# Two transformer blocks on one core: first tiles, turns, the RWKV chain and the bias map in another order, and five spare matmuls in each norm

## The chip, the cores and the metric

The kernel runs on one core of one Trainium2 chip. A core has a matrix engine (TensorE, PE in the profile), VectorE (DVE), ScalarE (ACT), GpSimd (POOL) and SyncE (SP), which here only issues transfers. Each engine works through its own list of instructions in order, and semaphores make one wait for another. The metric is the device time of one execution in microseconds; less is better.

## The reference

Two blocks in a row, on 256 tokens of width 1024, with fp32 inputs and outputs. The first block is of depth 2 and carries a second stream, 256 tokens of context, through nearly all of it. Cut to what matters here:

```python
def first_block(x, c, ctx, c_ctx, ...):
    h, hc = x, ctx
    for l in range(DEPTH):                     # DEPTH = 2
        # nine shift, scale and gate vectors for each stream: silu(c) @ w_ada[l] + b_ada[l]
        h = h + 0.5 * g1 * _swiglu(_modulate(_rms_norm(h, norm_ffn1[l]), sh1, sc1), ...)   # up1, down1
        # the same for hc
        u = _modulate(_rms_norm(h, norm_mix[l]), shm, scm)                                  # in
        # 16 heads: window, global and neighbourhood attention, each over its keys and the context's
        h = h + gm * (jnp.concatenate([y_w, y_g, y_n], axis=-1) @ w_out[l])                 # out
        h = h + 0.5 * g2 * _swiglu(_modulate(_rms_norm(h, norm_ffn2[l]), sh2, sc2), ...)   # up2, down2
    return _rms_norm(h, norm_final)

def second_block(x, positions, rel_bias, ...):
    h = _rmsnorm(x, norm_mix[l])
    p_rwkv, p_mla, p_diff, p_gate = jnp.split(h @ w_in[l], IN_SPLITS, axis=-1)
    o_rwkv = _rwkv7_mix(p_rwkv, ...)
    o_mla = _mla_mix(p_mla, ...)
    o_diff = _diff_mix(p_diff, positions, rel_bias, ...)
    x = x + merged @ w_o[l]                    # merged: the three, each by its gate
    x = x + _conv_ffn(_rmsnorm(x, norm_ffn[l]), ...)                                        # up_2, down_2
    return _rmsnorm(x, norm_final)

# inside _diff_mix
dist = positions[:, q0:q1, None] - positions[:, None, :q1]
bias = rel_bias[_t5_bucket(dist)]              # 32 buckets, 4 heads
logits = q @ k * scale + bias
```

## The kernel before, in words

**Weights.** Every fp32 product is made of three matmuls (`three`, L1083 to L1085) on operands that are split in a high and a low part: high by high, low by high, high by low. The weights come in panels of 128 x 2048 or less through one stream. SP issues the load of a panel (`Stream.load`), ACT writes the high part (`whi`, L537, in pieces L552 and L554), DVE the low part (`wlo`, L539, in pieces L560), PE multiplies. In places where PE works on attention a panel is split in quarters (`quarter`, L578, L592) between other instructions. `Stream.run` (L597) carries the phases up1, down1, up2, down2, w_o, up_2 and down_2: in each group of panels it evacuates the results of the group before, has the next panel split, and multiplies. The first panel of the next phase is split beside the last group. With `early` the second panel of a phase is taken to be split already by someone else.

**Norms.** `norm_scale` (L926) sums the squares over all features by matmuls with a table of ones (L937, L940), takes the root and the reciprocal, makes diagonal matrices of them (L956) and spreads these over all partitions by a matmul with ones (L964). `norm` (L981) then makes the normed operand `u` chunk by chunk (8 chunks of 128 features) as `u_hi` and `u_lo`. A chunk of both streams goes the wide way (L1017, L1044, L1047, L1052), the first chunk the slim way (L1009, L1025, L1035, L1036). PE starts on a chunk when its `u_lo` is there.

**In phases and attention of the first block.** `in_tile(i)` computes one output tile of `u @ w_in` over the 8 chunks; `program` runs them in an order with the attention of the heads between them. The results are evacuated by ACT from L1384 on. A list of heads' steps runs as generators, which are turned one step at a time. DVE's L1644 scales the probabilities; ACT and DVE prepare what PE multiplies. The w_out tiles follow at the end.

**The bias map.** The relative bias of the diff attention, a map of 128 x 4 heads x 384, is made by POOL alone in `bias_map` (L1224), from the list's place in layer 1 on: two DMAs (L1227, L1228), two casts, a distance (L1238), a start value (L1243), and for each of 31 bucket borders and 4 heads a pair: L1247 writes (distance >= border) x step into `bucket_step`, L1250 adds that to `rel_bias_map`. Each of the 248 instructions waits for the one before it. DVE adds the causal mask in L2227.

**Second block.** POOL's `load` (L1762) issues four DMAs: the tables, `w_a_g`, `pos_row_m` and, much later, `uq_ukv`. The RWKV part has three stages. First the chain (L1981 to L2189): token shifts, the small low-rank products, decay, norms of the keys, bonus, with DVE, ACT and PE handing each other small tiles; `v_tokens` (L2017) is the squared keys, whose sums over features PE makes in L2028; L2114 is the bonus. Its last DVE operation `e1` (L2189) starts the second stage, an inverse by six levels of small matmuls (L2184) with additions on DVE (L2220). Third, the scan over the chunks of the sequence (from L2291 on PE), which waits for a state set to zero by DVE (L2234). After the levels DVE does L2227, then L2234. In all of these stages `dense(n)` puts n quarter panels of side products, the panels of `w_in` for diff, MLA and gates, between the steps, so that PE has work while it waits. Their number is fixed: what is done early is missing at the end of the diff and MLA attention.

Nothing plans the order at run time: each engine's instructions stand in the order in which the program's functions are called.

## Time and profile before

| | us |
|---|---|
| median of 3 runs | 2553.18 (2553.05 to 2558.97) |
| the profiled execution | 2550.05 |
| its span, first to last instruction | 2548.7 |
| PE busy | 2408.7 (95%) |
| weight loads of PE busy | 1979.8 (78%) |
| DVE busy | 1210.2 (47%) |
| ACT busy | 970.3 (38%) |
| POOL busy | 441.2 (17%) |
| mean granted clock of PE | 0.972 of 2.4 GHz |

Places of the stages on the profile's time axis: attention of layer 0 from 500 to 700 us, norm and first in tiles of layer 1 from 1500 to 1525, attention of layer 1 from 1540 to 1700, up2 and down2 of layer 1 to 1926, norm to 1940, RWKV chain to 2037, levels to 2091, scan to 2131, diff and MLA attention to 2250, then gates and w_o to 2325, up_2 to 2471, down_2 to the end.

How to read it. A busy time of PE counts the time that matmuls are in the engine, so it holds no waiting but doesn't say whether they ran at full clock; the granted clock (1.00 is 2.4 GHz, 0.50 is 1.2 GHz) does. "Idle before" is the time for which an engine had nothing to do ahead of an instruction, and "<-" names what ended that wait. The chain is followed back from the last instruction, at each step to what released it.

### The profile page before, as it was taken

How to read it: one execution, taken by the hardware profiler on the slowest of the kernel's cores; microseconds unless marked ns; L12 is line 12 of the kernel's file. 1: busy time of each engine (PE TensorE's matmuls, PEld its weight loads, DVE VectorE, ACT ScalarE, POOL GpSimd, SP SyncE). 2: the span in 40 equal slices, each digit the busy share in tenths (PEclk: the TensorE clock that was granted, in tenths of full speed). 3: DMA queues.
4: the chain of work that ended last, by engine and by line, in shares of the span. 5: the costliest groups of instructions: out<-in, count | busy, mean ns of one | idle time of the engine just before them, and what ended most of it. 6: DMA issues, size and time to landing. Idle time of an engine off the chain costs nothing.

```text
span 2548.7 us, 38444 instructions
## 1 busy us (share of the span) xinstructions
PE 2408.7 (95%) x15464; PEld 1979.8 (78%) x15464; DVE 1210.2 (47%) x1797; ACT 970.3 (38%) x1540; POOL 441.2 (17%) x318
## 2 busy tenths in 40 slices
PE   7999999999999999999999989879988899998988
PEld 4777777666667777778888866669987897798988
DVE  4333222545653323243333346566655755676764
ACT  4222212455442222242222244345435324555762
POOL 1000000100000000000000039999994000000000
PEclk9999999899999999999999989999998899999999
DMA  7554455311034444323222241114544221244444
GB/s 281 209 182 176 160 200 184 97 50 50 34 132 168 179 177 164 136 85 115 90 92 84 96 117 67 66 67 158 178 148 143 84 105 55 84 149 149 170 151 141
DMA packets 51943, 329.51 MB, mean 129 GB/s; under 512 B 6480, under 2 KB 7504, under 8 KB 20976
## 3 DMA queue, kind: packets, MB, share of 16 engines
q1 hardware_dynamic: 48608, 318.46, 35.1%
q0 software_dynamic: 3216, 9.36, 1.3%
q8 instruction: 87, 1.43, 0.2%
q14 instruction: 32, 0.26, 0.0%
HBM read 323.99 MB, written 3.80 MB: 129 GB/s over the span
## 4 chain that ended last, share of the span: by engine, by line
PE 81%; DVE 8%; ACT 7%; issue 2%; DMA 2%; SPq 0%; ACTq 0%; DVEq 0%
PE bank L1083 24%; PE bank L1084 22%; PE bank L1085 22%; DVE wlo L539 2%; PE bank L825 2%; PE bank L1658 1%; PE bank L1591 1%; ACT sil L1044 1%; ACT whi L537 1%; PE bank L1680 1%; PE bank L2184 1%; DMA first_ada<-in_stream 1%; ACT u_hi L1047 1%; ACT probs L1628 1%; ACT probs_t L1665 1%
## 5 line engine op out<-in xcount | busy, mean ns | idle before, releaser
L1083 PE MATMUL bank<-u_hi,whi 128*128 128x512 f32 (+1 forms) x2512 | 882.3, 351 | 39.4 <-DVE wlo L539 13.2
L1084 PE MATMUL bank<-u_lo,whi 128*128 128x512 f32 (+1 forms) x2512 | 860.2, 342 | 0.0
L1085 PE MATMUL bank<-u_hi,wlo 128*128 128x512 f32 (+1 forms) x2512 | 858.5, 342 | 0.0
L1083 PEld LDWEIGHTS bank<-u_hi,whi 128*128 128x128 f32 x2512 | 485.8, 193 | 140.9 <-issue 50.6
L539 DVE TENSOR_TENSOR wlo<-raw,whi 128x2048 fp32r<-128x2048 f32 (+2 forms) x213 | 435.1, 2044 | 302.9 <-ACT whi L537 302.6
L1085 PEld LDWEIGHTS bank<-u_hi,wlo 128*128 128x128 f32 x2512 | 486.5, 194 | 53.1
L1084 PEld LDWEIGHTS bank<-u_lo,whi 128*128 128x128 f32 x2512 | 486.9, 194 | 47.8 <-issue 0.2
L537 ACT ACTIVATE whi<-raw 128x2048 fp32r<-128x2048 f32 (+2 forms) x213 | 360.9, 1695 | 171.1 <-PE bank L1085 118.2
L1145 ACT ACTIVATE sil<-bank 128x512 f32<-128x512 f32 (+1 forms) x88 | 47.9, 545 | 619.7 <-PE bank L1085 619.6
L1149 DVE TENSOR_TENSOR prod<-sil,bank 128x512 f32<-128x512 f32 (+1 forms) x88 | 54.7, 621 | 460.0 <-ACT sil L1145 456.9
L1247 POOL TENSOR_SCALAR bucket_step<-distance,bucket_steps 128x384 f32<-128x384 f32 x124 | 251.9, 2031 | 12.6
L1297 POOL DMA_DIRECT2D tables<-in_const x2 | 1.2, 580 | 1348.1 <-PE bank L1085 1348.1
L1083 PE MATMUL bank<-hidden_hi,whi 128*128 128x512 f32 x528 | 210.5, 399 | 0.0
L1085 PE MATMUL bank<-hidden_hi,wlo 128*128 128x512 f32 x528 | 208.4, 395 | 0.0
L1084 PE MATMUL bank<-hidden_lo,whi 128*128 128x512 f32 x528 | 208.3, 395 | 0.0
L1250 POOL TENSOR_TENSOR rel_bias_map<-rel_bias_map,bucket_step 128x384 f32<-128x384 f32 x124 | 146.8, 1184 | 10.3
L889 ACT ACTIVATE prod<-h 128x512 f32<-128x512 f32 (+3 forms) x63 | 33.4, 537 | 270.3 <-DVE h L1188 259.0
L560 DVE TENSOR_TENSOR wlo<-raw,whi 128x1024 fp32r<-128x1024 f32 (+1 forms) x70 | 89.1, 1280 | 75.9 <-ACT whi L552 63.1
L1083 PEld LDWEIGHTS bank<-hidden_hi,whi 128*128 128x128 f32 x528 | 99.3, 188 | 31.0 <-issue 7.4
L1085 PEld LDWEIGHTS bank<-hidden_hi,wlo 128*128 128x128 f32 x528 | 99.3, 188 | 23.6
L1084 PEld LDWEIGHTS bank<-hidden_lo,whi 128*128 128x128 f32 x528 | 99.3, 188 | 22.8
L1188 DVE SCALAR_TENSOR_TENSOR h<-bank,mod_g,h 128x256 f32<-128x256 f32 (+1 forms) x94 | 41.9, 479 | 128.1 <-PE bank L1085 128.0
(418 smaller groups left out, 2940.2 us busy)
## 6 DMA issues: line engine op xcount, KB each, us to landing
raw<-in_stream SPq DMA_DIRECT2D x231, 1024.0 KB, 4.8
raw<-in_stream SPq DMA_DIRECT2D x80, 704.0 KB, 4.0
first_ada<-in_stream SPq DMA_DIRECT2D x8, 1024.0 KB, 17.0
raw<-in_stream SPq DMA_DIRECT2D x8, 768.0 KB, 4.4
skew<-rpb_rows POOLq DMA_DIRECT2D x8, 336.0 KB, 6.6
nbr_bias<-skew POOLq DMA_DIRECT2D x24, 112.0 KB, 4.0
h<-in_tokens SPq DMA_DIRECT2D x1, 2048.0 KB, 12.0
uq_ukv<-in_small POOLq DMA_DIRECT2D x1, 1536.0 KB, 6.8
```

Source lines behind the costliest of these rows:

```text
L537: a.activation(self.hi[to][:, 0:n], raw[:, 0:n], ACT.Copy).then_inc(self.s_hi, 1)
L539: v.tensor_tensor(self.lo[to][:, 0:n], raw[:, 0:n], self.hi[to][:, 0:n].bitcast(F32), ALU.subtract).then_inc(self.s_lo, 1)
L560: r = v.q.tensor_tensor(self.lo[to][:, cols], self.raw[slot][:, cols], self.hi[to][:, cols].bitcast(F32), ALU.subtract)
L825: r = pe.q.matmul(banks[6][32 * q:32 * q + 32, 0:256], csil[:, 2 * k + i, :], weights[:, i * D + q * 256:i * D + q * 256 + 256], start=(k ...
L1083: pe.q.matmul(dst, w[0], x[0], start=start, stop=False)
L1084: pe.q.matmul(dst, w[0], x[1], start=False, stop=False)
L1085: return pe.q.matmul(dst, w[1], x[0], start=False, stop=stop)
L1145: act.q.activation(sil[par][:, 0:n], banks[2 * par][:, 0:n], ACT.Silu).then_inc(s_sil, 1)
L1149: dve.q.tensor_tensor(prod[par][:, 0:n], sil[par][:, 0:n], banks[2 * par + 1][:, 0:n], ALU.mult).then_inc(st.s_ev, 1)
L1188: r = dve.q.scalar_tensor_tensor(out=h[:, m, lo:hi], in0=bank[:, lo:hi], scalar=gate(s), in1=h[:, m, lo:hi], op0=ALU.mult, op1=ALU.add)
L1247: z = pool.do(pool.q.tensor_scalar(bucket[:, :], dist[:, :], float(start), steps[:, hh, b + 1:b + 2], ALU.is_ge, ALU.mult))
L1250: z = pool.do(pool.q.tensor_tensor(rel[:, hh, :], rel[:, hh, :], bucket[:, :], ALU.add))
```

## The change

1. **Loads.** SP issues `pos_row_m`, `w_a_g` and the tables, behind the first two panels of RWKV's `w_in`; POOL issued them before, behind the map. `uq_ukv` stays on POOL. All of SP's loads are put at the end of the program's text; their order on SP is otherwise as it was.
2. **Heads of down phases.** With `ahead`, the phase before splits the second panel in four pieces before its last evacuation; every down phase is `early`.
3. **Norms.** `stay_busy` puts matmuls on constants into a bank that nobody reads: 1 behind the sums of the kept squares, 1 behind the sums of the last ones, 3 behind the spreading matmuls, in 7 norms. In norms of two streams groups 0, 3 and 6 are slim, where only group 0 was.
4. **First tiles.** `first_tiles` runs the first two in tiles of a layer chunk by chunk side by side; the first side panel of the second block does the same.
5. **Bias map.** Its arithmetic starts only when the second panel of w_out in layer 1 is multiplied. The first 20 borders (80 pairs) stand there; the last 11 (44 pairs) are issued behind `e1`.
6. **RWKV chain.** The sines and cosines come first, the sigmoid ahead of the tanh, the key scaling `kk0` ahead of the decay's exponential, two of four reciprocals earlier, and five more quarters of dense work stand in the chain and at the beginning of the diff attention.

```diff
-    def load_rest(self):
+    def load_rest(self, second_block):
...
+            if ph.name == "rwkv_in":
+                second_block()
...
+        if ahead:
+            for piece in (0, 1, 2, 3):
+                self.split_piece(after, 1, piece)
         evacuate(Count(m), (g0 + m) % 2, Count(g0 + m), done)
...
+    def stay_busy(bank, times):
+
+        for _ in range(times if bank is not None else 0):
+            pe.q.matmul(banks[bank][:, 0:S], cst("ones"), const[:, 0:S], start=True, stop=True)
...
         for x in parts:
             sums(x, ssq, True, False)
+        stay_busy(spare, 1)
...
+        stay_busy(spare, 1)
         marks = [None, None]
         for x in parts:
             pe.after(scaled[x])
             marks[x] = pe.do(pe.q.matmul(banks[4 + x][:, 0:S], cst("ones"), diag[:, x * S:(x + 1) * S], start=True, stop=True))
+        stay_busy(spare, 3)
...
-            par, slim = x % 2, x < narrow
+            par, slim = x % 2, x < narrow or (streams == 2 and x % 3 == 0)
...
-        st.run(name, multiply, evacuate, ppg=2)
+        st.run(name, multiply, evacuate, ppg=2, early=True)
...
-        pool.after((s_pos, 32))
+        pool.after((s_pos, 32), (st.s_pe, PHASE[("out", L1 - 1)].first + 2))
...
-        for b, start in enumerate(bucket_starts()):
+        return bias_steps(z, 0, 20)
+
+    def bias_steps(z, lo, hi):
+
+        for b in range(lo, hi):
+            start = bucket_starts()[b]
             for hh in range(DH):
...
+        def first_tiles():
+
+            n = [q_cols(kind) for kind, _ in IN_TILES[0:2]]
+            places = [next_bank() for _ in n]
+            pe.q.wait_ge(st.s_lo, in_first + 1)
+            for kc in range(KC):
+                pe.after(ready[kc])
+                first = three(places[0][1][:, 0:n[0]], tile_of(in_first % 2, kc), chunk_of(u, kc, 0, n[0]), kc == 0, kc == KC - 1)
+                if kc == KC - 1:
+                    half_done = pe.do(first)
+                second = three(places[1][1][:, 0:n[1]], tile_of(in_first % 2, KC + kc), chunk_of(u, kc, 0, n[1]),
+                               kc == 0, kc == KC - 1)
+            second.then_inc(st.s_pe, 1)
...
-    tab2_ready = load(tab[:, :], ins["const"][:, CC.at["causal"]:CC.n], hidden_free)
...
+    def second_block_tables():
+        sp.wait_ge(*hidden_free)
+        sp.dma_start(prow[:, :], ins["pos_row"]).then_inc(s_row_pos, 16)
+        sp.dma_start(wag[:, :], ins["small"][:, SM_WA:SM_N]).then_inc(s_wag, 16)
+        sp.dma_start(tab[:, :], ins["const"][:, CC.at["causal"]:CC.n]).then_inc(s_tab2, 16)
...
+    trig_done = angles()
     for i in range(4):
         dense(2)
...
+    dve.after(*[mixed[c] for c in range(4, 8)])
+    for c in range(4):
+        kk0 = dve.do(dve.q.tensor_scalar(kk[:, c, :], K_[:, c, :], vcol("k_k", c), None, ALU.mult))
     act.after(sg)
-    trig_done = angles()
     dc = act.do(act.q.activation(flat4(dec[:, :, :]), flat4(dec[:, :, :]), ACT.Exp, scale=-float(np.exp(-0.5))))
...
     sqk = act.do(act.q.activation(flat4(vT[:, :, :]), flat4(kk[:, :, :]), ACT.Square))
-    dense(2)
-
+    dense(4)
...
+    dve.after(scanned, z1)
+    pinv = [dve.do(dve.q.reciprocal(by_chunk(dec[:, :, :])[:, c, :, :], Pb[:, c, :, 1:CH + 1])) for c in range(2)]
     dense(3)
...
     e1 = dve.do(dve.q.tensor_tensor(v16(TT[:, :, :]), ident_rows, v16(Mm), ALU.subtract))
+    pool.after(e1)
+    map_ready = bias_steps(map_ready, 20, NBUCKET - 1)
     dense(2)
...
-        dense(1 + i % 2)
+        dense(1 + i % 2 + (i < 2))
```

What stands in the engines' lists, at three places. Line numbers differ between the kernels, since the text has moved.

PE, the norm ahead of the in phase of layer 1, from its last sums to the first tile, before:

```order
L937 MATMUL bank<-const,prod 128x1
L937 MATMUL bank<-const,prod 128x1 [waits act_done]
L937 MATMUL bank<-const,prod 128x1
L964 MATMUL bank<-inv_norm_diagonal,const 128x256 [waits dve_done] x2
L1083 MATMUL bank<-u_hi,whi 128x256 [waits dve_done,weights_lo_done]
L1084 MATMUL bank<-u_lo,whi 128x256
L1085 MATMUL bank<-u_hi,wlo 128x256
L1083 MATMUL bank<-u_hi,whi 128x256 [waits dve_done]
L1084 MATMUL bank<-u_lo,whi 128x256
L1085 MATMUL bank<-u_hi,wlo 128x256
L1083 MATMUL bank<-u_hi,whi 128x256 [waits dve_done]
```

The tile's three matmuls of a chunk are followed by a wait for the next chunk.

PE at the same place in the changed kernel, where L933 is a spare matmul:

```order
L933 MATMUL bank<-const 128x256
L946 MATMUL bank<-const,prod 128x1 [waits act_done]
L946 MATMUL bank<-const,prod 128x1
L946 MATMUL bank<-const,prod 128x1 [waits act_done]
L946 MATMUL bank<-const,prod 128x1
L933 MATMUL bank<-const 128x256
L975 MATMUL bank<-inv_norm_diagonal,const 128x256 [waits dve_done] x2
L933 MATMUL bank<-const 128x256 x3
L1094 MATMUL bank<-u_hi,whi 128x256 [waits dve_done,weights_lo_done]
L1095 MATMUL bank<-u_lo,whi 128x256
L1096 MATMUL bank<-u_hi,wlo 128x256
L1094 MATMUL bank<-u_hi,whi 128x512
```

Spare matmuls (L933) stand ahead of, between and behind the norm's own, and the first chunk's three matmuls for one tile are followed by three for the second tile (128x512) before the next chunk is waited for.

POOL, the end of its list, before:

```order
L1250 TENSOR_TENSOR rel_bias_map<-rel_bias_map,bucket_step 128x384 [waits pool_done]
L1247 TENSOR_SCALAR bucket_step<-distance,bucket_steps 128x384 [waits pool_done]
L1250 TENSOR_TENSOR rel_bias_map<-rel_bias_map,bucket_step 128x384 [waits pool_done]
L1766 DMA tables_11689<-in_const 128x704 [waits panel_multiplied]
L1766 DMA w_a_g<-in_small 128x1024
L1766 DMA pos_row_m<-in_pos_row 128x256
L1766 DMA uq_ukv<-in_small 128x3072 [waits dve_done,act_done,pe_done]
```

The loads wait behind the map's last pair.

POOL in the changed kernel around the 81st pair, of which L1263 is the step of a bucket and L1266 its addition to the map:

```order
L1266 TENSOR_TENSOR rel_bias_map<-rel_bias_map,bucket_step 128x384 [waits pool_done]
L1263 TENSOR_SCALAR bucket_step<-distance,bucket_steps 128x384 [waits pool_done]
L1266 TENSOR_TENSOR rel_bias_map<-rel_bias_map,bucket_step 128x384 [waits pool_done]
L1263 TENSOR_SCALAR bucket_step<-distance,bucket_steps 128x384 [waits pool_done,dve_done]
L1266 TENSOR_TENSOR rel_bias_map<-rel_bias_map,bucket_step 128x384 [waits pool_done]
```

The 81st pair waits for DVE (`dve_done`, which stands for `e1`); three of the four loads have left POOL's list, and the last one stands behind the map as before.

DVE, the end of the levels and the beginning of the scan, before:

```order
L2220 TENSOR_TENSOR inverse_t<-inverse_t,bank 128x512
L2227 TENSOR_TENSOR rel_bias_map<-rel_bias_map,tables_11689 128x4x128 [waits tokens_loaded,constants_loaded,pool_done]
L2227 TENSOR_TENSOR rel_bias_map<-rel_bias_map,tables_11689 128x4x128
L2234 MEMSET sil 128x256 [waits dve_done]
L539 TENSOR_TENSOR wlo<-raw,whi 128x2048 [waits weights_hi_done]
```

The map is added to right behind the last level.

DVE at the same place in the changed kernel:

```order
L541 TENSOR_TENSOR wlo<-raw,whi 128x2048 [waits weights_hi_done]
L2258 TENSOR_TENSOR inverse_t<-inverse_t,bank 128x512 [waits pe_done]
L2258 TENSOR_TENSOR inverse_t<-inverse_t,bank 128x512
L2265 TENSOR_TENSOR rel_bias_map<-rel_bias_map,tables_10966 128x4x128 [waits tokens_loaded,constants_loaded,pool_done]
L2265 TENSOR_TENSOR rel_bias_map<-rel_bias_map,tables_10966 128x4x128
L2275 MEMSET sil 128x256 [waits dve_done]
```

The two additions to `rel_bias_map` wait for POOL in both kernels, stand at the same place, and the memset of the state and the next split of weights stand behind them.

## Rows read from the trace of the kernel before

**Rows 1.** the page, busy times and the chain that ended last, by engine.
```profile
PE 2408.7 (95%) x15464; PEld 1979.8 (78%) x15464; DVE 1210.2 (47%) x1797; ACT 970.3 (38%) x1540; POOL 441.2 (17%) x318
...
PE 81%; DVE 8%; ACT 7%; issue 2%; DMA 2%; SPq 0%; ACTq 0%; DVEq 0%
```

**Rows 2.** stretches: us, busy us (x instructions), PE clock, DMA share, GB/s.
```profile
1730.00:1853.00 123.00, 123.00 (x1028) 123.00 (x1027) 74.11 (x66) 53.02 (x66) 117.07 (x65) 1.00 0.51 180
1940.00:2037.00 97.00, 81.91 (x793) 78.26 (x793) 65.20 (x120) 42.61 (x70) 3.39 (x5) 0.88 0.30 109
2037.00:2091.00 54.00, 54.00 (x1148) 51.93 (x1145) 27.60 (x30) 15.09 (x21) 0.00 (x0) 1.00 0.22 76
```

**Rows 3.** timeline of POOL, 1505 to 1521 us: start, duration, instruction [idle before <-releaser].
```profile
1513.27 0.73 POOL L1231 CAST bucket_step<-pos_row 128x256 f32<-128x256 int32 x1 [3.54 <-DMA pos_col<-in_pos_col]
...
1520.24 1.58 POOL L1247 TENSOR_SCALAR bucket_step<-distance,bucket_steps 128x384 f32<-128x384 f32 x1
```

**Rows 4.** instruction groups, POOL, 1520 to 1942 us: busy, mean | idle.
```profile
L1247 POOL TENSOR_SCALAR bucket_step<-distance,bucket_steps 128x384 f32<-128x384 f32 x124 | 251.9, 2031 | 12.6
L1250 POOL TENSOR_TENSOR rel_bias_map<-rel_bias_map,bucket_step 128x384 f32<-128x384 f32 x124 | 146.8, 1184 | 10.3
```

**Rows 5.** groups of instructions, POOL, 1598 to 1609 us.
```profile
L1247 POOL TENSOR_SCALAR bucket_step<-distance,bucket_steps 128x384 f32<-128x384 f32 x4 | 6.3, 1582 | 0.4
L1250 POOL TENSOR_TENSOR rel_bias_map<-rel_bias_map,bucket_step 128x384 f32<-128x384 f32 x4 | 4.0, 1002 | 0.3
```

**Rows 6.** groups of instructions, POOL, 1730 to 1853 us.
```profile
L1247 POOL TENSOR_SCALAR bucket_step<-distance,bucket_steps 128x384 f32<-128x384 f32 x33 | 76.0, 2304 | 3.4
L1250 POOL TENSOR_TENSOR rel_bias_map<-rel_bias_map,bucket_step 128x384 f32<-128x384 f32 x32 | 42.5, 1327 | 2.7
```

**Rows 7.** timeline of DVE, 2089.8 to 2093.2 us.
```profile
2091.10 1.29 DVE L2227 TENSOR_TENSOR rel_bias_map<-rel_bias_map,tables 128x512 f32<-128x512 f32 x2
```

**Rows 8.** timeline of PE at the end of w_out's second panel, layer 1.
```profile
1696.01 0.28 PE L1085 MATMUL bank<-y_hi,wlo 128*128 128x256 f32 x1
```

**Rows 9.** timeline of DVE at e1, 2036 to 2037.3 us.
```profile
2036.13 1.23 DVE L2189 TENSOR_TENSOR inverse_t<-tables,mixed 128x1024 f32<-128x1024 f32 x1
```

**Rows 10.** groups of instructions, DVE, 1730 to 1853 us.
```profile
L539 DVE TENSOR_TENSOR wlo<-raw,whi 128x2048 fp32r<-128x2048 f32 (+1 forms) x21 | 48.9, 2331 | 26.8 <-ACT whi L537 26.8
L1128 DVE TENSOR_TENSOR hidden_x_lo<-prod,hidden_x_hi 128x256 f32 (+1 forms) x22 | 17.6, 798 | 0.5 <-ACT hidden_x_hi L1126 0.5
```

**Rows 11.** groups of instructions, DVE, 2037.36 to 2091.1 us.
```profile
L539 DVE TENSOR_TENSOR wlo<-raw,whi 128x2048 fp32r<-128x2048 f32 x4 | 9.2, 2289 | 5.5 <-ACT whi L537 5.5
...
L2178 DVE TENSOR_TENSOR mixed<-chunk_products,tables 128x1024 f32<-128x1024 f32 x5 | 6.1, 1224 | 6.9 <-PE bank L2184 6.9
```

**Rows 12.** groups of instructions, PE, 1503 to 1525 us.
```profile
L1083 PE MATMUL bank<-u_hi,whi 128*128 128x256 f32 (+1 forms) x18 | 8.8, 487 | 7.6 <-DVE u_lo L1052 5.6 <-DVE u_lo L1036 2.1
```

**Rows 13.** busy time of the engines in three stretches at a lower clock.
```profile
1503.00:1525.00 22.00, 14.95 (x53) 11.68 (x54) 12.21 (x21) 14.00 (x27) 17.31 (x24) 0.61 0.50 112
1974.00:1985.00 11.00, 9.91 (x48) 9.94 (x49) 7.43 (x24) 5.49 (x9) 0.00 (x0) 0.53 0.00 1
2005.00:2015.00 10.00, 6.65 (x24) 5.64 (x23) 9.93 (x20) 0.09 (x1) 0.00 (x0) 0.50 0.29 107
```

**Rows 14.** timeline of PE, head of the down phase of layer 1.
```profile
1857.19 0.39 PE L1083 MATMUL bank<-hidden_x_hi,whi 128*128 128x256 f32 x1 [2.08 <-DVE wlo L539]
```

**Rows 15.** timeline of PE, head of the last down phase.
```profile
2476.25 0.58 PE L1083 MATMUL bank<-hid,whi 128*128 128x256 f32 x1 [4.92 <-DVE wlo L539]
```

**Rows 16.** groups of instructions, PE, 1969.1 to 1978.6 us.
```profile
L2028 PE MATMUL bank<-const,v_tokens 128*128 128x2 f32 x16 | 3.5, 351 | 6.1 <-ACT v_tokens L2017 6.1
```

**Rows 17.** groups by shape, DVE, attention of layer 1, 1540 to 1700 us.
```profile
L1644 DVE TENSOR_SCALAR probs<-probs,stat 128x512 f32<-128x512 f32 x32 | 21.3, 707 | 0.6
```

**Rows 18.** groups by shape, DVE, attention of layer 0, 500 to 700 us.
```profile
L1644 DVE TENSOR_SCALAR probs<-probs,stat 128x512 f32<-128x512 f32 x32 | 14.1, 483 | 0.6
```

**Rows 19.** groups of instructions, PE, 1926 to 1940 us, a norm.
```profile
L964 PE MATMUL bank<-inv_norm_diagonal,const 128*128 128x256 f32 x4 | 1.8, 584 | 0.6 <-DVE inv_norm_diagonal L956 0.6
```

82 lines of the change are left out of this document (41 added, 41 removed).

## The prediction

> **What bounds the kernel now.** I read the page's busy times and its chain first [rows 1]. TensorE (PE) is busy 95% of the span and holds 81% of the chain that ended last; VectorE (DVE) holds 8% and ScalarE 7%. So time can be gained only where PE waits or runs at its lower clock, and it is lost wherever another engine makes PE wait longer. GpSimd (POOL) is busy 17%, and all of that matters little today. Then I read the stretches [rows 2]: from 1730 to 1853 us PE has no gap and POOL works beside it almost without a pause; from 1940 to 2037, the RWKV chain, PE is busy 82 of 97 us at clock 0.88; from 2037 to 2091, the inverse by levels, PE is full and POOL does nothing. The change puts POOL work into exactly that last stretch, so I next followed POOL's bias map.
>
> The map is built by 124 pairs (31 buckets x 4 heads) of L1247 and L1250, each instruction waiting for the one before. They start at 1520.24 [rows 3] and end at 1941.8, and with the idle time before them they take 251.9 + 146.8 + 12.6 + 10.3 = 421.6 us, 3.40 us a pair [rows 4]. The rate differs by place: with little on DVE a pair takes (6.3 + 4.0 + 0.4 + 0.3) / 4 = 2.75 us [rows 5]; with DVE busy 60% it takes (76.0 + 42.5 + 3.4 + 2.7) / 32.5 = 3.83 us [rows 6]. The first reader of the map is DVE's L2227, which starts at 2091.10 [rows 7]. Before, the map is ready 149 us ahead of it.
>
> **The map.** The changed kernel starts the map when the second w_out panel of layer 1 is multiplied, 1696.01 + 0.28 = 1696.3 [rows 8]. Setup takes 1520.24 - 1513.27 = 7.0 us [rows 3], so pairs start at about 1703. Eighty pairs at 3.40 to 3.83 us take 272 to 306 us and end at 1975 to 2009. The 81st pair waits for DVE's e1 (L2189), which ends at 2036.13 + 1.23 = 2037.4 [rows 9]; even if what follows moves e1 forward by 20 us, POOL will mostly be standing idle there, for 10 to 60 us.
> From e1 on 44 pairs remain, and DVE's L2227 stands 2091.10 - 2037.36 = 53.7 us behind it. Both instants shift together, so this distance is what the map can hide in. In it DVE is busy 51% [rows 2], close to the stretches that give the mean of 3.40; I take that: 53.7 / 3.40 = 15.8 pairs are covered. The other 28.2 run while DVE is stopped at L2227 with its split of the weights queued behind it, so PE soon has nothing either. They run at the free rate of 2.75 us: **78 us**. The bounds: all 44 at the free rate, 44 x 2.75 - 53.7 = 67 us; the slow rate of 3.83 for the covered part, (44 - 53.7 / 3.83) x 2.75 = 82 us, and 85 at 4.1 us a pair in the covered part, a little above [rows 6]. Queued behind L2227 on DVE are the state's memset and every weight split; PE's scan waits for the memset, so PE stops after the two quarter panels of dense work placed ahead of the scan. PE comes back from a 70 us pause at its lower clock, which costs 3 us (1 to 4), taken from the stretches below in which it restarts at 0.50 to 0.53.
>
> The row on which a rule can be weighed: POOL spends 118.5 us on 32.5 pairs where it would need 32.5 x 2.58 = 84, thus 35 us lost, beside DVE instructions with two inputs in on-chip memory that are busy 48.9 + 17.6 = 66.5 us [rows 6, 10]. The Trainium skill, SBUF — State Buffer, section "Who interferes with whom", says that such a DVE instruction and a GpSimd one that reads this memory share a port pair which is an exclusive lock, and that the later one blocks fully. By a full lock POOL would have lost up to 66.5 us; the trace shows about half, so it agrees in kind and not in size. By the full rule the DVE instructions of that sort among the levels, 9.2 + 6.1 = 15.3 us [rows 11], would leave 38.4 us or 14 pairs, and a stall of 83 us instead of 78; by the half that the trace shows, 75 us.
>
> **What it gains.**
> In-phases. The first two tiles are interleaved chunk by chunk, so that each normed chunk feeds two tiles. In layer 1 PE stands 7.6 us between 1503 and 1525 waiting for u_lo [rows 12] and runs at 0.61 [rows 13]. I take 11 us over both layers and the RWKV head (8 to 14), since the work of the second tile, some 6 us a layer, goes into gaps.
> Heads of the down phases. Their first panel now is split ahead. PE waits 2.08 us for wlo at 1857.19 [rows 14] and 4.92 at 2476.25 [rows 15], 7.0 in all, and comes back with matmuls of 0.39 and 0.58 us against 0.28 before the pause; with that restart and layer 0: 10 us (7 to 11).
> RWKV chain. PE waits 6.1 us for ACT's v_tokens [rows 16] and then runs at 0.53 from 1974 to 1985, later at 0.50 from 2005 to 2015 [rows 13]. The busy time there, 9.9 + 6.7, would be half at full clock. So 6.1 + 8.3 = 14.4 is at stake, with a short wait beside it, and a few more quarters of dense work and earlier tables and reciprocals go there: 15 us (6 to 20). The five quarters are taken from the end of the diff and MLA attention, where fewer remain as cover: 0 (-5 to +4).
> Attention of layer 1. Without POOL beside it DVE's L1644 takes 483 ns, as in layer 0, and not 707 [rows 17, 18]: 32 x 0.22 = 7.2 us of DVE time, and as much again in its other lines. PE idles there more than in layer 0 and runs at a lower clock; I take 7 us (0 to 14).
> Norms. Spare matmuls, 35 in all, keep PE busy while it waits; one is like L964, 584 ns at the low clock [rows 19]. Most lie in time that is idle; the three behind the broadcast can delay the first real matmul by up to 1.5 us a norm. Together with the slimmer groups: 5 us (-4 to +13).
> The DMAs moved from POOL to SP, w_a_g, tables_2 and pos_row_m, would arrive before 1950 as before: 0. The uq_ukv load now stands behind the map, at its end, and is wanted only in the diff and MLA part, over 40 us later: 0.
> The sum: 11 + 10 + 15 + 7 + 5 = 48 us gained; 78 + 3 = 81 us lost; net +33 us. On the profiled 2550.05 us (a span of 2548.7) that is 2583; the profiled run stood 3.1 us under the median of 2553.18, so on the median I forecast **2586 us**.
>
> **The rivals.**
> 1. The gains mostly don't come (spare matmuls delay real ones, the chain still waits for v_tokens, the clock falls anyway). Against it: the waits named are plain and their releasers are moved earlier. With 20 us gained: 2553 + 81 - 20 = 2614.
> 2. The gains are at their upper ends and the rest of the map runs at its free rate: 67 + 2 - 65 = +4, some 2557 to 2563. For it: each removed wait also keeps the clock up. Against it: the terms would all have to go the same way.
> 3. The map is hidden after all, and the kernel is faster. The mechanism: from e1 to L2227, the 44 pairs fit, so that only the gains count, 2553 - 48 = 2505. It decides at 53.7 / 44 = 1.22 us a pair; L1247 alone takes 1.58 where it is free [rows 5]. It could only be so if DVE's wait were met earlier than the last pair, and the order of instructions shows it behind pool_done. A weaker form, where the wait is passed on and the pause is then given back by weights that are already split and loaded, can return no more than a few us, since PE is 95% busy.
> 4. The 81st pair comes late because POOL has not finished the first 80 at e1. At 4.1 us a pair (above [rows 6]) they end at 2031, and with e1 earlier by 20 us that adds up to 14 us: 2600. For it: DVE is busy 67% of the RWKV chain [rows 2]. Against: the mean rate leaves 28 us of room.
>
> **Chances.** Forecast, with rival 4's smaller part: 0.60, its own range 2571 to 2602. Rival 1: 0.16. Rival 4 in full: 0.06. Rival 2: 0.11, of which 0.03 falls within 0.3% (7.7 us, about what a measurement can tell) and 0.02 below. Rival 3: 0.04. Something between the forecast and 2560 for other reasons: 0.03, counted as slower. This gives slower 0.90, same 0.04, faster 0.06. The range reaches from 2559 to 2614; it takes in the bounds of the stall (67 to 85) with gains of 25 to 62.
>
> **What would show it.** In the changed kernel's trace: POOL starts at 1690 to 1700 and not at 1513; its 81st pair starts right after DVE's e1 with an idle time of 10 to 60 us released by DVE; DVE has an idle time of 70 to 85 us before the first rel_bias_map add, released by POOL; PE has one pause of about 70 us or more before the scan, the longest of the kernel; L1644 in layer 1 takes about 480 ns; the wait for v_tokens falls below 3 us; the waits for wlo at the heads of the down phases are gone. The forecast is wrong if the pause before the scan is under 50 us, which would mean that the pairs run faster among the levels than anywhere now, or if it is there and the total is nonetheless under 2560, which would mean gains that I have undercounted.

## The result and the profile after

| | before | after |
|---|---|---|
| median | 2553.11 us (4 runs) | 2620.99 us (2619.91 to 2621.96, 4 runs) |
| profiled execution | 2550.05 | 2621.4 |
| its span | 2548.7 | 2620.1 |
| mean granted clock of PE | 0.972 | 0.965 |

The ratio is 1.0263, with a 95% interval of 1.0244 to 1.0281: 67 us slower. I had forecast 2586 and a range of 2559 to 2614. The direction is right, the size is half of what it was, and the time lies outside the range.

The page of the changed kernel, its busy times and the chain that ended last, which answer to [rows 1]:

```profile
PE 2416.7 (92%) x15534; PEld 1984.7 (76%) x15534; DVE 1200.3 (46%) x1822; ACT 962.3 (37%) x1534; POOL 435.4 (17%) x315
...
PE 75%; DVE 9%; ACT 7%; POOL 5%; issue 2%; DMA 1%; ACTq 0%; DVEq 0%; SPq 0%; POOLq 0%
```

POOL was in no place of the chain before and now holds 5% of it. Where, the windows show, which answer to [rows 2]: the RWKV norm and chain (111 us before, 1926 to 2037), the levels, and what follows them.

```profile
1908.00:2028.00 120.00, 95.98 (x882) 90.72 (x883) 81.43 (x138) 51.09 (x88) 60.21 (x41) 0.86 0.27 96
2028.00:2083.00 55.00, 54.82 (x1148) 52.71 (x1144) 29.42 (x30) 14.92 (x20) 51.92 (x32) 1.00 0.22 79
2083.00:2162.00 79.00, 0.93 (x8) 0.72 (x6) 2.34 (x4) 0.00 (x0) 73.16 (x58) 0.53 0.04 13
```

In the last 79 us PE is busy 0.9 us and POOL 73. That is the stop that I had forecast. DVE's and PE's timelines show both ends of it (start, duration, instruction, idle time before it and what ended that):

```profile
2160.82 1.29 DVE L2265 TENSOR_TENSOR rel_bias_map<-rel_bias_map,tables 128x512 f32<-128x512 f32 x2 [76.66 <-POOL rel_bias_map L1266]
2162.11 0.27 DVE L2275 MEMSET sil<- 128x256 f32 x1
```

PE's timeline at the first matmul of the scan:

```profile
2162.53 0.38 PE L2332 MATMUL bank<-v_tokens,chunk_products 64*64 64x64 f32 x2 [78.60 <-DVE sil L2275]
```

DVE waits 76.66 us for POOL's last pair and PE 78.60 us for the memset behind it; [rows 7] had no wait. POOL's own timeline shows that the arithmetic starts at 1680.29 and not at 1513.27 [rows 3]:

```profile
1680.29 0.40 POOL L1242 CAST bucket_step<-pos_row 128x256 f32<-128x256 int32 x1 [173.06 <-PE bank L1096]
```

The same view at the 81st pair, which starts at `e1` after 56.31 us of idle time:

```profile
2028.22 4.59 POOL L1263 TENSOR_SCALAR bucket_step<-distance,bucket_steps 128x384 f32<-128x384 f32 x1 [56.31 <-DVE inverse_t L2225]
```

POOL's groups of instructions for the first 80 pairs (busy, mean ns | idle before), which answer to [rows 4]:

```profile
L1263 POOL TENSOR_SCALAR bucket_step<-distance,bucket_steps 128x384 f32<-128x384 f32 x80 | 165.3, 2066 | 8.1
L1266 POOL TENSOR_TENSOR rel_bias_map<-rel_bias_map,bucket_step 128x384 f32<-128x384 f32 x80 | 104.5, 1306 | 6.7
```

And for the last 44:

```profile
L1263 POOL TENSOR_SCALAR bucket_step<-distance,bucket_steps 128x384 f32<-128x384 f32 x44 | 76.0, 1726 | 60.7 <-DVE inverse_t L2225 56.3
L1266 POOL TENSOR_TENSOR rel_bias_map<-rel_bias_map,bucket_step 128x384 f32<-128x384 f32 x44 | 48.6, 1104 | 3.7
```

The first 80 take (165.3 + 104.5 + 8.1 + 6.7) / 80 = 3.56 us each and are done 56.3 us before e1 ends. The last 44 take 76.0 + 48.6 + (60.7 - 56.3) + 3.7 = 132.7 us, 3.02 each: from e1's end at 2028.2 to the levels' end at 2084.2 DVE gives 56.0 us of cover, and 132.7 - 56.0 = 76.7 us remain.

So the stop came as worked out (78 us). What did not come are the gains. To read them I compared the times at which the profiled executions of the two kernels reach the same instruction. The changed kernel is ahead by 5.6 us at the first attention, 2.5 at the norm before in of layer 1 (1501.2 to 1498.7), 16.3 at the norm after w_out, 19.6 at the norm before RWKV, and then only 9.2 at e1 and 7.0 at the last level. At the end it is 71.4 behind: 78.6 for the stop and less than 8 gained. Inside the chain PE stands still for 22.3 us, in four places, each time waiting for split weights (the shortest, 1.85 us, is not shown). Its timeline at the first:

```profile
1935.13 0.58 PE L1094 MATMUL bank<-u_hi,whi 128*128 128x256 f32 x1 [8.09 <-DVE wlo L541]
```

At the second, which begins 36 us after the end of the first:

```profile
1978.59 0.58 PE L1094 MATMUL bank<-u_hi,whi 128*128 128x256 f32 x1 [7.56 <-DVE wlo L541]
```

And at the last, behind the bonus:

```profile
2002.39 0.58 PE L1094 MATMUL bank<-u_hi,whi 128*128 128x256 f32 x1 [4.82 <-DVE wlo L541]
```

The wait for `v_tokens` [rows 16] has indeed shrunk, from 6.1 to 0.27 us, and the waits for weights have taken its place.

### The profile page after: what moved, and what is told of

It is laid out like the page before. It is cut to its first block, busy times and chain, and to the rows that moved or that the text cites. A ratio compares the mean times of both kernels' runs of the same rounds, so it can differ in the third digit from the quotient of the medians.

```text
span 2620.1 us, 38607 instructions
## 1 busy us (share of the span) xinstructions
PE 2416.7 (92%) x15534; PEld 1984.7 (76%) x15534; DVE 1200.3 (46%) x1822; ACT 962.3 (37%) x1534; POOL 435.4 (17%) x315
## 4 chain that ended last, share of the span: by engine, by line
PE 75%; DVE 9%; ACT 7%; POOL 5%; issue 2%; DMA 1%; ACTq 0%; DVEq 0%; SPq 0%; POOLq 0%
PE bank L1094 22%; PE bank L1095 21%; PE bank L1096 21%; POOL bucket_step L1263 3%; PE bank L829 3%; DVE wlo L541 2%; POOL rel_bias_map L1266 2%; PE bank L1693 1%; ACT sil L1056 1%; PE bank L1715 1%; PE bank L1626 1%; ACT whi L539 1%; ACT u_hi L1059 1%; DMA first_ada<-in_stream 1%; ACT probs L1663 1%
## 5 line engine op out<-in xcount | busy, mean ns | idle before, releaser
L541 DVE TENSOR_TENSOR wlo<-raw,whi 128x2048 fp32r<-128x2048 f32 (+2 forms) x208 | 426.9, 2053 | 305.5 <-ACT whi L539 305.3
L539 ACT ACTIVATE whi<-raw 128x2048 fp32r<-128x2048 f32 (+2 forms) x208 | 354.3, 1703 | 175.0 <-PE bank L1096 127.1
L1263 POOL TENSOR_SCALAR bucket_step<-distance,bucket_steps 128x384 f32<-128x384 f32 x124 | 241.2, 1946 | 68.8 <-DVE inverse_t L2225 56.3
L1266 POOL TENSOR_TENSOR rel_bias_map<-rel_bias_map,bucket_step 128x384 f32<-128x384 f32 x124 | 153.0, 1234 | 10.3
L562 DVE TENSOR_TENSOR wlo<-raw,whi 128x1024 fp32r<-128x1024 f32 (+2 forms) x80 | 92.1, 1171 | 97.5 <-ACT whi L554 81.8
```

The lines of the kernel that those rows point to most:

```text
L539: a.activation(self.hi[to][:, 0:n], raw[:, 0:n], ACT.Copy).then_inc(self.s_hi, 1)
L541: v.tensor_tensor(self.lo[to][:, 0:n], raw[:, 0:n], self.hi[to][:, 0:n].bitcast(F32), ALU.subtract).then_inc(self.s_lo, 1)
L562: r = v.q.tensor_tensor(self.lo[to][:, cols], self.raw[slot][:, cols], self.hi[to][:, cols].bitcast(F32), ALU.subtract)
L1263: z = pool.do(pool.q.tensor_scalar(bucket[:, :], dist[:, :], float(start), steps[:, hh, b + 1:b + 2], ALU.is_ge, ALU.mult))
L1266: z = pool.do(pool.q.tensor_tensor(rel[:, hh, :], rel[:, hh, :], bucket[:, :], ALU.add))
```

## The experiments

All ratios are to the kernel before on the same chip, with 95% intervals.

### The map alone, and the rest alone

**map_on_before**: the map's two edits in the kernel before.

```diff
-        pool.after((s_pos, 32))
+        pool.after((s_pos, 32), (st.s_pe, PHASE[("out", L1 - 1)].first + 2))
...
+    pool.after(e1)
+    map_ready = bias_steps(map_ready, 20, NBUCKET - 1)
```

> The kernel before with the change to the bias map alone: arithmetic from w_out's second panel on, the last 44 pairs behind e1. Theory A, the stopped pairs alone make the loss and their price adds to the rest: DVE waits 76 to 80 us for POOL before the first rel_bias_map add, some 6 us are lost in levels, restart and scan, some 6 are gained in layer 1's attention where POOL is gone: 2553 + 78 + 6 - 6 = 2631, 2622 to 2638. Theory B, part of the 77 us pause in the changed kernel was given back by work done ahead and the loss comes from elsewhere: under 2610.

Measured: 2659.46 us, 1.0421 (1.0405 to 1.0437), above what either theory gave. The stop is there with nearly the same length, as DVE's timeline shows:

```profile
2197.51 1.29 DVE L2234 TENSOR_TENSOR rel_bias_map<-rel_bias_map,tables 128x512 f32<-128x512 f32 x2 [78.62 <-POOL rel_bias_map L1255]
```

But there is a second one. PE's groups of instructions between 1945 and 1985:

```profile
L1991 PE MATMUL bank<-mixed,w_a_g 64*128 64x256 f32 x8 | 3.8, 648 | 32.8 <-issue 32.8
```

And POOL's timeline just behind the 80th pair:

```profile
1976.91 0.55 POOL L1771 DMA_DIRECT2D w_a_g<-in_small  x1
```

PE stands 32.8 us until `w_a_g` is there: the profile names no releaser ("issue"), but the load lands 4.1 us after it was issued, at 1981.0, and PE goes on at 1981.2. The load stands on POOL's list behind the first 80 pairs, which now end at 1976 and not at 1942. In the changed kernel SP issues this load at 1906.5, and PE does not wait for it. The move of the loads to SP, which I had booked at 0, thus belongs to the map's move: without it the 32.8 us come on top.

**map_early**: the changed kernel with the map's arithmetic where and as it was. **late_whole**: the start at w_out kept, the gate at e1 taken away.

```diff
# map_early; late_whole keeps the first line of "-"
-        pool.after((s_pos, 32), (st.s_pe, PHASE[("out", L1 - 1)].first + 2))
+        pool.after((s_pos, 32))
...
-        return bias_steps(z, 0, 20)
+        return bias_steps(z, 0, NBUCKET - 1)
...
-    pool.after(e1)
-    map_ready = bias_steps(map_ready, 20, NBUCKET - 1)
```

> The changed kernel with the map's arithmetic as it was before (from in layer 1's list on, all 124 pairs in one piece, no wait for e1). Theory A: no wait of DVE for POOL; 2621 - 77 - 6 + 6 = 2544, 2539 to 2550, so faster than before by 0.3 to 0.4 per cent only, since the RWKV chain gives nothing. Theory B, the other parts gain the 48 us that I forecast and something else is lost with the map: 2505 to 2520.

> The changed kernel with the map in one piece from w_out's second panel on, no wait for e1, the reader where it is. In the changed kernel POOL stands 56.3 us at e1; without that the 44 pairs move into the chain, where they run at 3.4 to 3.8 us. Theory A, the gate costs what it takes from POOL: the map ends at 1687 + 124 x 3.5 = 2121, some 37 us behind the levels' end at 2084: 2621 - 77 + 37 = 2581, 2572 to 2590. Theory B, POOL beside the chain slows DVE as much as it hides: over 2600.

Measured: map_early 2547.24 us, 0.998 (0.9971 to 0.9989); late_whole 2577.69 us, 1.0095 (1.0077 to 1.0113). Theory A held in both. The map's late start and gate together cost (1.0263 - 0.998) x 2553 = 72 us, what the late start gains in the attention taken off, and all other parts together gain 5 us. DVE's timeline of late_whole at the map's reader:

```profile
2119.73 1.29 DVE L2263 TENSOR_TENSOR rel_bias_map<-rel_bias_map,tables 128x512 f32<-128x512 f32 x2 [29.90 <-POOL rel_bias_map L1266]
```

Of the 76.7 us, 46.8 are therefore the gate's and 29.9 the late start's. In total 43 us went with the gate.

**add_late26**: 26 borders before e1, 5 behind it, and the first reader moved behind the scan.

```diff
-    dve.after(map_ready, tab2_ready, loaded)
-    for o in (0, 2 * P):
-        rel_ready = ...
...
+    dve.after(map_ready, tab2_ready, loaded)
+    for o in (0, 2 * P):
+        rel_ready = ...
     dve.after(rel_ready, lam_ready, scan_over)
```

> The changed kernel with 26 of the 31 borders before e1 and 5 behind it, and the causal mask added to the map (the first reader) only before the diff attention, behind the scan. Theory A, the loss is only that the reader stands before the last pair: no pause before the scan; 20 pairs at 2.8 to 3.4 us end 56 to 68 us behind e1, long before the diff attention: 2621 - 77 - 4 = 2540, 2534 to 2547, at or under map_early. Theory B, POOL's pairs beside the DVE work of the chain and the scan cost as much as beside the attention: 2545 to 2555.

Measured: 2548.05 us, 0.9984 (0.9975 to 0.9993). The stop is gone: the last pair ends at 2119.5, and the reader, which now stands behind the scan, starts at 2138.3. Two things were changed here, the reader's place and six more borders ahead of e1, and no run has the first alone. By my estimate it would not do: 44 pairs of 3.02 us from e1's end at 2034.8 on would end at 2168, 30 us behind that reader. And the kernel is no faster than map_early, though it is 15.9 us ahead of the kernel before at the norm after w_out and map_early only 5.4. By e1 that is down to 2.5 against 3.9. Theory B is nearer.

### The RWKV chain

**chain_back_map_early**: map_early with the chain of before.

```diff
-    trig_done = angles()
     for i in range(4):
...
     act.after(sg)
+    trig_done = angles()
...
-    pinv = [...reciprocal... for c in range(2)]
...
-    dense(5)        # and 3, 4, and (i < 2) in the diff attention
+    dense(4)        # and 2, 3, without (i < 2)
```

> As map_early, and the RWKV chain of before in it: sines behind the decay's sigmoid, tanh ahead of sigmoid, kk0 late, all four reciprocals behind bb, the quarters of dense work as before. Theory A, the new order of the chain is what costs there (in the changed kernel PE stands still 8.1, 7.6, 1.9 and 4.8 us in it, 22.3 in all, against 15.1 before): 10 to 20 us faster than map_early, 2524 to 2534. Theory B, the late weights come from the loads that SP now issues behind the end of down2: no faster than map_early, 2540 to 2548, and e1 no earlier than in it.

Measured: 2531.34 us, 0.9918 (0.9905 to 0.9932), as theory A had it. The new chain costs 16 us. Four kernels divide that.

**angles_late** puts back the place of the sines alone, **rest_back** all but that, **quarters_back** the numbers of quarters alone:

```diff
# angles_late, on map_early
-    trig_done = angles()
     for i in range(4):
...
     act.after(sg)
+    trig_done = angles()
# quarters_back, on map_early (rest_back has this too)
-    dense(5)
+    dense(4)
...
-            dense(3)
+            dense(2)
...
-    dense(4)
+    dense(3)
...
-        dense(1 + i % 2 + (i < 2))
+        dense(1 + i % 2)
```

> map_early with one thing put back: the sines and cosines behind the decay's sigmoids, as before. Theory A, the early sines are the main cost of the new chain: ACT stands 8.0 us at the first sine until DVE has the angles, its split of the third RWKV panel waits behind that, and PE stands 8.1 us for it. 2547 - 8 to 12 = 2535 to 2539. Theory B, the dense work, the reciprocals and kk0 cost it: 2544 to 2548.

> map_early with the other things of the chain put back (tanh first, kk0 late, four reciprocals behind bb, the quarters of dense work in the chain and in the attentions as before) and the sines still first. Theory A as above: 2547 - 3 to 6 = 2541 to 2544. Theory B: 2532 to 2537.

> map_early with the five quarters of dense work alone put back (4, 2 and 3 in the chain instead of 5, 3 and 4, and none extra in the first two units of the diff attention); sines, kk0 and two reciprocals stay early. Theory A, the quarters cost the 15 us between map_early (2547) and rest_back (2532): a quarter needs a weight panel that DVE has split, and in the chain DVE is the engine that is behind, so PE waits for wlo: 2531 to 2536. Theory B, the two reciprocals (1.7 us each on DVE, ahead of the norm of the keys) cost it: 2543 to 2548. In between, both share.

Measured: angles_late 2546.15 us, 0.9976 (0.9967 to 0.9985); rest_back 2532.07 us, 0.9919 (0.9905 to 0.9932); quarters_back 2536.26 us, 0.993 (0.9917 to 0.9944). My theory of the sines fell: their place is worth 1 us. They do make a pause: with them first, PE waits 7.95 us for the third panel (rest_back), because ACT stands at the first sine until DVE has the angles, and its split of the weights is behind that. With them late, PE waits 6.06 us for `v_tokens` (chain_back_map_early). One wait is exchanged for another. PE's timeline of rest_back:

```profile
1942.36 0.58 PE L1094 MATMUL bank<-u_hi,whi 128*128 128x256 f32 x1 [7.95 <-DVE wlo L541]
```

And of chain_back_map_early:

```profile
1963.26 0.56 PE L2066 MATMUL bank<-const,v_tokens 128*128 128x2 f32 x2 [6.06 <-ACT v_tokens L2052]
```

The quarters are 11 to 13 of the 15 us (by the medians and by the ratios). **three_more** adds only three quarters to the good chain:

```diff
-    dense(4)
+    dense(5)
...
-            dense(2)
+            dense(3)
...
-    dense(3)
+    dense(4)
```

> chain_back_map_early (2531) with nothing but three more quarters of dense work in the chain, 5, 3 and 4 instead of 4, 2 and 3. Theory A, the quarters alone are the cost: PE must wait for panels that DVE has not split, and e1 comes some 7 us later, with 2 to 4 us more behind it: 2538 to 2543. Theory B, they cost only together with the early sines and reciprocals: 2529 to 2534.

Measured: 2542.45 us, 0.9959 (0.9945 to 0.9972), 11 us over chain_back_map_early. Theory A. The window from the norm to e1, in chain_back_map_early:

```profile
1921.00:2026.00 105.00, 88.13 (x833) 82.81 (x834) 75.25 (x138) 49.60 (x85) 17.49 (x12) 0.89 0.30 108
```

And in three_more:

```profile
1917.00:2030.00 113.00, 93.52 (x878) 88.79 (x880) 75.86 (x136) 51.25 (x87) 26.52 (x16) 0.88 0.27 98
```

PE's waits for split weights in these windows (us in total, times, longest), chain_back_map_early:

```profile
PE bank L1094 <- DVE wlo L541: 6.6, 2, 4.5
```

three_more:

```profile
PE bank L1094 <- DVE wlo L541: 10.4, 4, 4.8
```

The chain is 8 us longer, 113 against 105 (the profiled execution of chain_back_map_early was the slowest of its five, but slim_back, which has the same chain, takes 104 us from 1918 to 2022). PE does 5.4 us more work in it (93.5 to 88.1), the three quarters, and waits 3.8 us more for weights; its idle time as a whole is 2.6 us longer. Not every such wait is DVE's: in both kernels one is for a panel whose load was late, while DVE stood still (2.7 us of wait in three_more, 4.5 in chain_back_map_early). The wait that is new is the last. DVE's timeline of three_more just before it ends:

```profile
2001.46 0.88 DVE L1914 SCALAR_TENSOR_TENSOR mixed<-shifted,vec,mixed 128x256 f32<-128x256 f32 x2
2002.25 2.29 DVE L541 TENSOR_TENSOR wlo<-raw,whi 128x2048 fp32r<-128x2048 f32 x1
```

And PE's, which that split releases:

```profile
2004.59 0.58 PE L1094 MATMUL bank<-u_hi,whi 128*128 128x256 f32 x1 [4.82 <-DVE wlo L541]
```

DVE comes to this split straight from the chain's own operations, without any idle time. From the `v_tokens` matmuls to e1 it splits six panels in three_more and five in chain_back_map_early, 2.29 us each. The work is not saved later: from e1 to the norm behind w_o both kernels lose 2 to 3 us on the kernel before. Thus quarters put into this chain cost their own time on PE and a split on DVE. That PE takes them in one piece, so that what the chain's next step needs from PE comes so much later, fits this but was not tested by itself.

### The single gains

**first_back**, **ahead_back**, **slim_back** and **no_spare** each take one part out of chain_back_map_early.

```diff
# first_back
-            yield from first_tiles()
-            for i in range(2, len(IN_TILES)):
+            for i in range(len(IN_TILES)):
... (and the order of the second block's first side panel)
# ahead_back
-        st.run(name, multiply, evacuate, finish_hidden(n, hidden, h0), early=name != ("up1", 0), ahead=True)
+        st.run(name, multiply, evacuate, finish_hidden(n, hidden, h0), early=name != ("up1", 0))
...
-        st.run(name, multiply, evacuate, ppg=2, early=True)
+        st.run(name, multiply, evacuate, ppg=2)
... (and the same for up_2 and down_2)
# slim_back
-            par, slim = x % 2, x < narrow or (streams == 2 and x % 3 == 0)
+            par, slim = x % 2, x < narrow
# no_spare
-        for _ in range(times if bank is not None else 0):
+        for _ in range(0):
```

> chain_back_map_early (2531) with the first two tiles of both in phases and of the RWKV panel one after the other again. Forecast was 11 us: 2540 to 2544. By the milestones in the traces the kernel is 5.6 us ahead at the first attention and keeps 2 of it at its end, some 6 us in layer 1: theory A 2537 to 2541. Theory B, the attention behind takes nearly all: 2532 to 2536.

> chain_back_map_early (2531) without the split ahead of the down phases' second panel. Forecast was 10 us: 2538 to 2543. By the milestones (3 us at down2 of layer 1, 4.5 at the last down phase, nothing in layer 0) theory A 2537 to 2540; theory B, the pieces delay the last evacuation and give half back: 2533 to 2536.

> chain_back_map_early (2531) with only group 0 slim in the norms of two streams. Theory A, slim groups shorten the wait for the first chunks in the two norms that feed interleaved tiles: 2533 to 2536. Theory B, no difference: 2529 to 2533.

> chain_back_map_early (2531) without the 35 spare matmuls. Theory A, they pay by keeping the clock up behind each norm: 2 to 8 us slower, 2533 to 2539. Theory B, what they save in clock they cost in the time of the first chunk's matmuls: 2529 to 2533. Theory C, they cost: 2523 to 2528.

| taken out | median | ratio, 95% interval | worth by the ratios |
|---|---|---|---|
| nothing (chain_back_map_early) | 2531.34 | 0.9918 (0.9905 to 0.9932) | |
| first tiles | 2546.21 | 0.9978 (0.9969 to 0.9987) | 15 us |
| split ahead | 2540.35 | 0.9948 (0.9935 to 0.9961) | 8 us |
| slim groups | 2533.36 | 0.9921 (0.9907 to 0.9935) | not to be told from 0 |
| spare matmuls | 2530.60 | 0.9916 (0.9902 to 0.9929) | not to be told from 0 |

Measured against what was expected, first_back lies above every range given (2532 to 2544), ahead_back within its forecast and just above theory A, slim_back between its two theories, no_spare in theory B. The four gains add up to 23 us, where the kernel gains 21.

The spare matmuls do what they are there for, and within the noise, about 3 us here, it is worth nothing. The window of the norm and first tiles of layer 1 without them:

```profile
1500.00:1520.00 20.00, 16.33 (x77) 12.97 (x78) 16.09 (x28) 16.40 (x31) 15.92 (x22) 0.83 0.50 124
```

And with them, in chain_back_map_early:

```profile
1500.00:1520.00 20.00, 15.73 (x83) 11.32 (x82) 16.04 (x29) 16.18 (x31) 16.29 (x23) 1.00 0.58 131
```

The clock is 0.83 without them and 1.00 with them. Two things stand against it in this window: 1.5 us of PE's 15.73 are the spare matmuls themselves, and PE waits 4.1 us for normed chunks with them and 3.6 without, since the chunks come from DVE and ACT. Which of the two takes the gain was not tested.

**pool_loads** and **chain_pool_loads** put the three loads back on POOL, in map_early and in chain_back_map_early.

```diff
-    def second_block_tables():
-        sp.wait_ge(*hidden_free)
-        sp.dma_start(...)                      # pos_row_m, w_a_g, tables
...
+    tab2_ready = load(tab[:, :], ins["const"][:, CC.at["causal"]:CC.n], hidden_free)
...
+    wag_ready = load(wag[:, :], ins["small"][:, SM_WA:SM_N], hidden_free)
...
+    pr_ready = load(prow[:, :], ins["pos_row"], hidden_free)
```

> map_early (2547) with the three loads issued by POOL behind the map again, as before. Theory A, with the map done by 1941 they arrive in time either way: 2545 to 2549. Theory B, SP's wait for the end of down2 holds back the stream's panels and is part of the RWKV loss: 2540 to 2544.

> chain_back_map_early (2531) with the three loads on POOL behind the map, as before. pool_loads lost 11.5 us against map_early, with a pause of 20.8 us in which PE waited for the third RWKV panel behind the early sines. Theory A, that was the sines' need of pos_row_m alone: here 2529 to 2533. Theory B, w_a_g arrives too late as well: 2535 to 2545.

Measured: pool_loads 2558.76 us, 1.0026 (1.0016 to 1.0036); chain_pool_loads 2547.14 us, 0.9975 (0.9964 to 0.9986). They cost 12 and 15 us. Both kernels are slower than any range that I gave; theory A fell in both, pool_loads went the other way from its theory B, and in chain_pool_loads the cause that theory B named was found. PE's timeline of pool_loads at its longest wait in the chain:

```profile
1958.08 0.58 PE L1094 MATMUL bank<-u_hi,whi 128*128 128x256 f32 x1 [20.78 <-DVE wlo L541]
```

And of chain_pool_loads, at the first use of `w_a_g`:

```profile
1949.08 0.76 PE L2024 MATMUL bank<-mixed,w_a_g 64*128 64x256 f32 x1 [8.61 <-issue]
```

POOL ends the map at 1941 to 1944 in these two as in the kernel before. In chain_pool_loads `w_a_g` is issued at 1944.2 and lands 4.7 us later, and PE starts at 1949.08. In pool_loads `pos_row_m` is issued at 1942.2, the first sine starts at 1949.9, after 20.9 us in which ACT has nothing, and the split of the third panel stands behind it. Once the other engines are 10 us earlier, a load behind the map is late, and the 10 us are given back.

**late_map_chain_back** was the attempt to keep POOL off the attention: the late start, 23 borders before e1, the reader behind the scan, the good chain (add_late26's and chain_back_map_early's edits, with 23 for 26).

> The changed kernel with the chain of before, 23 borders ahead of e1 and 8 behind it, and the causal mask added only before the diff attention. Theory A, POOL off layer 1's attention gives 10 us at w_out (16.3 ahead of before there, against 5.4 in map_early), and 92 pairs end near e1, so that the chain stays undisturbed; 32 pairs from e1 take 88 to 109 us and just reach the diff attention, 100 us behind it: 2531 - 10 + 2 = 2523, 2518 to 2528. Theory B, the chain is DVE's and POOL beside it takes the 10 us back: 2529 to 2535.

Measured: 2538.58 us, 0.9948 (0.9935 to 0.9962), 7 us slower than chain_back_map_early and slower than theory B's range. It is 16.1 us ahead of the kernel before at the norm after w_out, 19.4 before RWKV, and 14.4 at e1. The window of its chain, to be held against chain_back_map_early's above:

```profile
1911.00:2024.00 113.00, 88.79 (x870) 83.85 (x869) 90.79 (x134) 48.95 (x83) 97.57 (x64) 0.85 0.25 94
```

With POOL busy for 97.6 us beside it DVE is busy 90.8 us, for the work that takes 75.3 where POOL is busy for 17.5. DVE's instructions don't all suffer. Two of its groups in late_map_chain_back, a reciprocal, which has one operand in on-chip memory, and a product of two such operands:

```profile
L2116 DVE RECIPROCAL decay<-decay_products 128x256 f32<-128x256 f32 x4 | 7.0, 1741 | 0.0
L2127 DVE TENSOR_TENSOR decayed_kk_r<-decay_products,kk 128x256 f32<-128x256 f32 x4 | 3.6, 889 | 0.0
```

And in chain_back_map_early:

```profile
L2116 DVE RECIPROCAL decay<-decay_products 128x256 f32<-128x256 f32 x4 | 7.0, 1745 | 0.0
L2127 DVE TENSOR_TENSOR decayed_kk_r<-decay_products,kk 128x256 f32<-128x256 f32 x4 | 1.7, 421 | 0.0
```

DVE also waits 4.2 us for the last of the 32 pairs at the reader behind the scan. The cause of theory B was there, and its price was higher than I gave: from the norm before RWKV to e1 this kernel loses 5.1 us on the kernel before, and chain_back_map_early gains 3.3. POOL's pairs beside the chain thus cost 8 us. From e1 to the norm behind w_o it loses 5.3 us more than chain_back_map_early, the 4.2 us of the reader among them, so that nothing is left of what POOL's absence gains in the attention.

The fastest kernels are thus chain_back_map_early and its like (2531 us, 0.9918): the change without its new bias map and RWKV chain, 21 us faster than before.

## Why the prediction was wrong

**The stop: right.** 80 pairs at 3.40 to 3.83 us, measured 3.56; POOL idle 10 to 60 us at e1, measured 56.3; 15.8 pairs covered and 28.2 at 2.75 us, 78 us, measured 76.7 by DVE's wait and 78.6 by PE's (map_early has 1.9 of the latter too). Between the map's reader and the norm behind w_o the changed kernel loses 2.2 us more than map_early, which I put down to the restart: 79 us in all, forecast 81. The 72 us by the ratios are this less what the late start gains (forecast 81 - 7 = 74). map_on_before has the stop too. One reading was wrong, and without effect: the room of 28 us that rival 4 calls the mean rate's is that of the slow rate of 3.83 us; the mean rate of 3.40 leaves 62. And the chances of a slower kernel add up to 0.91, not 0.90. Rival 3 needed pairs of 1.22 us and is out.

On the port rule, DVE's groups of two-input instructions in the 56 us among the levels, now with POOL beside them:

```profile
L541 DVE TENSOR_TENSOR wlo<-raw,whi 128x2048 fp32r<-128x2048 f32 x5 | 11.9, 2374 | 9.8 <-ACT whi L539 9.8
L2214 DVE TENSOR_TENSOR mixed<-chunk_products,tables 128x1024 f32<-128x1024 f32 x5 | 6.7, 1340 | 4.9 <-PE bank L2220 4.7
```

They are busy 11.9 + 6.7 = 18.6 us. POOL is busy 53.0 us on 33 instructions of which a pair needs 2.58 us unhindered, so it lost 53.0 - 16.5 x 2.58 = 10 us, about half. The Trainium skill (SBUF — State Buffer, "Who interferes with whom") speaks of a full block for the whole instruction; the trace agrees in kind, and POOL's loss is again smaller than by the full rule. DVE loses too (L2127 above), so the half need not speak against a lock; no run here separates that. The stop of 76.7 lies between the 75 us by half a lock and my 78, not at the 83 by the full rule.

**In-phases: under by 4.** Forecast 11 us (8 to 14), first_back shows 15.

**Heads of the down phases: right.** Forecast 10, within bounds of 7 to 11; ahead_back shows 8. The waits are not all gone, as I had said they would be: PE's timeline of the changed kernel at the head of the last down phase has 2.37 us where [rows 15] had 4.92:

```profile
2552.66 0.38 PE L1094 MATMUL bank<-hid,whi 128*128 128x256 f32 x1 [2.37 <-DVE wlo L541]
```

**RWKV chain: this is the step that failed.** I wrote that 14.4 us were at stake and that "a few more quarters of dense work and earlier tables and reciprocals go there: 15 us (6 to 20)". Measured: -16 us, a miss of 31; and the 15 were already more than the 14.4 at stake. The wait for `v_tokens` went as said, but I counted it as gained without asking what was late next. It was the split of the third panel, which stands behind the sines on ACT. And I took more dense work for a filler of idle time. three_more shows that it is an addition to the chain: 5.4 us of work and a new wait of 4.8 us for a panel that DVE splits between the chain's own operations, a chain 8 us longer and a kernel 11 us slower, with nothing back at the end, where I had booked the same quarters at 0. [rows 2] had a warning in it: DVE is busy 65 of 97 us in the chain, and the quarters' weights pass through DVE.

**Attention of layer 1: the mechanism right, the gain kept in part.** L1644, which is L1679 now, takes 484 ns and no longer 707 [rows 17, 18]. DVE's groups by shape in the attention of layer 1:

```profile
L1679 DVE TENSOR_SCALAR probs<-probs,stat 128x512 f32<-128x512 f32 x32 | 14.1, 484 | 0.6
```

At the norm behind w_out the changed kernel is 10.9 us further ahead than map_early (16.3 to 5.4). But the pairs then lie beside the chain and slow DVE there: at e1, and still at the last level, 5.3 us are left (9.2 to 3.9, 7.0 to 1.7), 5 and not 7. With more pairs ahead of e1 nothing is left, and add_late26 is no faster than map_early (0.9984 to 0.998). I had moved POOL's work without pricing it where it went.

**Norms: 0 and not +5**, by no_spare and slim_back, to within some 3 us each. The price was read too low as well: a spare matmul stands in the trace as two rows, like each matmul of [rows 19] (70 rows of L933 for 35 matmuls), so its price is about twice what I took.

**The loads: a 0 that was none.** They cost nothing where they are now, but left on POOL they would have cost 12 to 15 us of the gains ahead of 1941, and 33 us with the map's move (map_on_before).

The sum then: 48 us forecast, minus 31 (chain), 2 (attention) and 5 (norms), plus 4 and minus 2 for the first two terms, is 12 us gained; 2553 + 79 - 12 = 2620. The terms were measured in different kernels, so a few us in it are luck; without the attention's 5 they make 7, and map_early shows 5. Of the 35 us by which I missed, the chain alone is 31. Rival 1, gains that mostly don't come, was the true one, and its 2614 still gave them 20 us. Its reasons were mostly not: the chain no longer waited for v_tokens, and the clock did not fall (0.86 in the norm and chain, 0.85 before from 1926 to 2037). In place of the old waits came new ones.

## What to carry to other kernels

Before work of an engine that has time is moved, look for its first reader in every list it feeds: a wait that had 149 us of slack stopped the whole kernel for 77 when 44 pairs were gated behind a late instruction. With the reader behind the scan and 24 of the 44 pairs ahead of the gate the stop was gone. When a wait is taken out, ask which queue is next to be late, above all the weight splits that share ACT and DVE with the chain; and filler work in a stretch that another engine bounds is no filler if it uses that engine too. A load that stands behind long work on its engine is on time only as long as nothing else gets faster.
